# The rows of an expert tile placed in slots four apart

## The reference

```python
g_sel = argmax(t @ rc_w + rc_b)                  # one of 4 groups
lf_sel = (t @ rf_w + rf_b)[g_sel]                # 8 experts of that group
vals, idx = top_k(softmax(lf_sel), 2)            # two of them
for e in range(32):
    h = silu(t @ w_gate[e]) * (t @ w_up[e])      # (536, 512)
    out = out + gates[:, e:e + 1] * (h @ w_down[e])
```

## Time and profile before

| what | value |
|---|---|
| median of three runs | 1102.85 us |
| lowest and highest | 1101.57 and 1104.02 us |
| the profiled execution's own time | 1102.73 us |
| its span, first to last instruction | 1100.9 us |
| mean granted TensorE clock | 0.966 |
| TensorE matmul busy | 992.9 us (90%) |
| VectorE, ScalarE, GpSimd busy | 441.0, 311.5, 330.2 us |
| DMA moved | 277.54 MB, 252 GB/s over the span |

### The profile page before, as it was taken

The page is one execution under the profiler, slowest core; times in us unless marked ns, Lnnn a source line. Parts: engine busy times, 40 slices in busy tenths (PEclk is TensorE's granted clock), DMA queues, the critical chain, the costliest instruction groups (busy, mean ns, idle before and its releaser), DMA issues.

```text
span 1100.9 us, 16994 instructions
## 1 busy us (share of the span) xinstructions
PE 992.9 (90%) x6438; PEld 701.5 (64%) x6439; DVE 441.0 (40%) x674; ACT 311.5 (28%) x597; POOL 330.2 (30%) x534
## 2 busy tenths in 40 slices
PE   6999989999999999999999999999977778998881
PEld 5889768876876587999765555555544434554440
DVE  6999874353435699963151111111101011111103
ACT  3026222453202625322242222222212121221223
POOL 1000888888012994000012222222221111221210
PEclk9999999999979899999989999999989999999996
DMA  6684261110529643327299999999999999999954
GB/s 259 124 146 74 42 141 40 39 60 20 62 79 264 235 150 132 136 96 296 111 359 377 395 392 390 384 393 408 399 393 409 381 421 411 411 417 414 423 237 162
DMA packets 73564, 277.54 MB, mean 252 GB/s; under 512 B 36952, under 2 KB 38872, under 8 KB 56496
## 3 DMA queue, kind: packets, MB, share of 16 engines
q1 hardware_dynamic: 63020, 252.67, 62.6%
q0 software_dynamic: 8720, 19.86, 6.6%
q10 hardware_dynamic: 1780, 4.41, 1.1%
HBM read 260.17 MB, written 25.61 MB: 260 GB/s over the span
## 4 chain that ended last, share of the span: by engine, by line
PE 54%; DMA 22%; DVE 17%; SPq 3%; issue 2%; ACT 1%; POOLq 0%; ACTq 0%; POOL 0%; DVEq 0%
DMA sb_arena<-w_up 16%; PE ps L650 11%; PE ps L1015 8%; PE ps L1008 7%; PE ps L1029 7%; PE ps L912 7%; DVE sb_arena L1386 6%; DMA sb_arena<-w_gate 4%; SPq L407 2%; PE ps L982 2%; PE ps L769 2%; PE ps L795 1%; PE ps L820 1%; PE ps L738 1%; PE ps L816 1%
## 5 line engine op out<-in xcount | busy, mean ns | idle before, releaser
L650 PE MATMUL ps<-sb_arena 128*128 128x264 f32 (+1 forms) x1152 | 273.1, 398 | 14.7 <-DMA sb_arena<-wi 13.8
L650 PEld LDWEIGHTS ps<-sb_arena 128*128 128x128 f32 x1152 | 222.1, 194 | 65.9 <-DMA sb_arena<-wi 13.9
L1889 DVE TENSOR_TENSOR sb_s5b<-sb_s5b,ps 128x256 f32<-128x256 f32 x36 | 22.4, 623 | 414.4 <-PE ps L1015 414.4
L1015 PE MATMUL ps<-sb_arena 128*64 128x256 f32 x1152 | 134.5, 387 | 21.3 <-DMA sb_arena<-w_up 21.3
L1008 PE MATMUL ps<-sb_arena 128*64 128x256 f32 x1152 | 134.3, 387 | 19.1 <-DMA sb_arena<-w_gate 15.0
L1029 PE MATMUL ps<-sb_arena 128*64 128x512 f32 x576 | 131.5, 598 | 20.6 <-DVE sb_arena L1893 20.6
L1008 PEld LDWEIGHTS ps<-sb_arena 128*64 128x64 f32 x1152 | 84.3, 139 | 79.7 <-DMA sb_arena<-w_gate 24.4
L1015 PEld LDWEIGHTS ps<-sb_arena 128*64 128x64 f32 x1152 | 83.6, 139 | 68.3 <-DMA sb_arena<-w_up 27.4
L1359 ACT ACTIVATE sb_kxf<-ps,sb_gate_of 64x512 f32<-64x512 f32 x36 | 24.6, 682 | 304.9 <-PE ps L1029 304.9
L1029 PEld LDWEIGHTS ps<-sb_arena 128*64 128x64 f32 x576 | 39.0, 136 | 90.0 <-issue 61.0
L606 POOL COPY sb_idc<-sb_tok_of 64x1 int32 x36 | 6.4, 178 | 288.5 <-DMA sum_scr<-sb_kxf,sb_rwc 272.4
(11 more groups left out here) (306 smaller groups left out, 1275.0 us busy)
## 6 DMA issues: line engine op xcount, KB each, us to landing
sb_arena<-w_gate SPq DMA_DIRECT2D x32, 2048.0 KB, 32.0
sb_arena<-w_up SPq DMA_DIRECT2D x32, 2048.0 KB, 34.0
sb_arena<-w_down SPq DMA_DIRECT2D x32, 2048.0 KB, 34.3
sb_arena<-wi SPq DMA_DIRECT2D x28, 512.0 KB, 4.1
sb_arena<-w_out SPq DMA_DIRECT2D x4, 2048.0 KB, 8.3
sb_arena<-wglu SPq DMA_DIRECT2D x8, 512.0 KB, 4.6
sb_arena<-ssm_in POOLq DMA_DIRECT2D x8, 512.0 KB, 15.3
o_ssm_s<-sb_arena POOLq DMA_DIRECT2D x8, 512.0 KB, 4.9
```

The lines of the kernel that those rows point to most:

```text
L650: last = mm(ps[:, b0 + h, 0:t1 - t0], ring[w % 3][:, k, :], src[:, k, t0:t1], start=k == 0, stop=k == KD - 1)
L1015: last = mm(ps[64 * r:64 * r + 64, 1, 0:256], xt[:, k, :], Wu[s][:, k, 256 * r:256 * r + 256], start=k == 0, stop=k == KD - 1)
L1889: V.tensor_tensor(hh.rearrange("p (j c) -> p c j", j=2), sg.rearrange("p (c j) -> p c j", j=2), ps[:, 1, 0:256].rearrange("p (c j) -> p c ...
```

## The change

Row r of a tile no longer sits in slot r, but in slot 4 (r mod 16) + r div 16: rows 0, 1, 2, ... 15 in slots 0, 4, 8, ... 60, rows 16 to 31 in slots 1, 5, ... 61, and so on. Only the two comparisons that make `oh_row` are changed. The row number is now compared with a list that is read in another order: the constants 0..63 viewed as (4, 16) and transposed, so that column 4 w + e of the one-hot is compared with 16 e + w. The tokens, the gates and the first tile follow, because all three are products with `oh_row`. The instructions of every engine are the same in number, kind, size and order; what differs is the step of one operand of two VectorE instructions (64 bytes instead of 4 between neighbours), and which of the 64 slots are empty.

```diff
             flat = lambda v: v.rearrange("p i k -> p (i k)")
             io64 = cst[:, C_IO:C_IO + T]
-            tt(oh_row, bc(flat(slf), 2, T), bc(io64, 1, 10), ALU.is_equal)
+            spread = lambda v: v.rearrange("p a (w e) -> p a w e", e=T // 16)
+            row_no = bc(io64.rearrange("p (e w) -> p w e", w=16), 1, 10)
+            rows_at = lambda: tt(spread(oh_row), spread(bc(flat(slf), 2, T)), row_no, ALU.is_equal)
+            rows_at()
             both = oh_row.rearrange("p (i k) t -> p i k t", k=2)
             V.tensor_tensor(oh0, both[:, :, 0], both[:, :, 1], ALU.add).then_inc(oh_first, 1)
             dv.wait_ge(oh_first, 1)
...
             stt(slf, stf, -float(T), slf, ALU.mult, ALU.add)
-            tt(oh_row, bc(flat(slf), 2, T), bc(io64, 1, 10), ALU.is_equal)
+            rows_at()
             tt(oh_tile, bc(flat(stf), 2, IDXC), bc(io64[:, 0:IDXC], 1, 10), ALU.is_equal)
```

## The result

The time after is 1105.81 us (median of 11 runs, 1102.70 to 1108.28), against 1101.98 us for the kernel before (11 runs on the same chip, 1099.32 to 1104.02). The ratio is 1.0033 with a 95% interval of 1.0023 to 1.0044, so the change costs 3.6 us (2.5 to 4.8), the ratio times 1,102 us. The whole interval lies above the 0.2% that a measurement can tell: **slower**, as forecast. The profiled execution took 1105.92 us, with a span of 1104.0 us (before: 1102.73 and 1100.9).

A forecast was written before the change was run, and what follows sets the result against it. The most loaded DMA engine was taken to bound the kernel. 1102.73 us plus 5.2 for ten more rows, minus 0.3 for the last scatter, VectorE and GpSimd 0, gave 1107.6 us; range 1102.5 to 1111.5 us.

The forecast's parts named there:

- The bound: Expert loop: TensorE goes at the pace of the most loaded DMA engine; engines finish up to 22 us apart.
- The mapping: Gathers and scatters: engine g has slots 2g, 2g + 1, 2g + 32, 2g + 33; the last two inferred.
- The price: Token-row packets in the expert loop: ten more rows on the most loaded engine cost 5.2 us, between 3.2 and 5.6.
- Where the time is lost: Expert loop: engine 0 behind from the start, 15.4 us against TensorE's 12.47; longer late periods at 17 to 33 rows.
- The step to a half: End of the loads: DMA share falls in one large step to about 0.5 and stays for 25 us or more.
- VectorE: Two comparisons with a strided operand: 0 us taken, covered by queued loads; 0.7 us kept for the range.
- GpSimd: Waits for scatters in the loop: about 0.6 us longer in tiles of 17 to 32 rows, covered, 0 us.
- The last scatter: End of the kernel: 7 rows on seven engines, one each, so the second round goes away, -0.3 us.
- The sum: Whole kernel: profiled execution plus rows minus last scatter, 1102.73 + 5.2 - 0.3 = 1107.6 us.
- Rival 1: Gathers and scatters: slots in blocks of four on an engine, so the change levels the load; -11.9 us; chance 0.08.
- Rival 2: Expert loop: fewer engines on rows at once hurt weights less, giving back 5 us, so no change; chance 0.12.
- Rival 3: Loop: rows 5.6 us, first comparison 0.7, TensorE's lower clock up to 2, so 1111 us; inside the forecast's range.

The follow-up runs named there:

- level order: Against the kernel before: row r of a tile dealt to engine r mod 16, one row to an engine in turn; 1095.48 us, ratio 0.9933.
- reversed back half: Against the kernel before: rows 0 to 31 keep their slots, the pairs of rows 32 to 63 are put in reverse order; 1092.99 us, ratio 0.9912.
- level, turned on: Against the kernel before: row r of tile t sits where the level order puts row r + 3t, modulo 64; 1091.71 us, ratio 0.9905.
- slots of the change, turned on: Against the kernel before: row r of tile t sits where the change puts row r + 27t, modulo 64; 1091.64 us, ratio 0.9908.
- the last two experiments: Against the kernel before: the slots of the change turned on from tile to tile, 1091.64 us; and the reversed back half, 1092.99 us.

## Why the prediction was right, and where it was not exact

All runs together, in the order of the most loaded engine. The change against before is the ratio times 1,102 us; "loop" is the one profiled execution, first gate product to last down product. That execution is not always a typical one: it lay 4.2 us under its median for the level order and 3.9 us above it for the reversed back half, so these two loops can't be compared with each other; the others lay within 1.5 us of theirs.

| order | greatest load, rows | against before, us | 95% interval | loop, us |
|---|---|---|---|---|
| four neighbours on one engine | 140 | +23.3 | +21.2 to +25.3 | 522.8 |
| slots of the change | 109 | +3.6 | +2.5 to +4.8 | 503.4 |
| the same, plain operand | 109 | +3.7 | +2.4 to +5.0 | 503.6 |
| before | 99 | | | 498.0 |
| slots of before, strided operand | 99 | -0.4 | -2.3 to +1.3 | 497.6 |
| level in the tile | 86 | -7.4 | -9.1 to -5.5 | 490.8 |
| back half reversed | 81 | -9.7 | -12.1 to -7.2 | 492.8 |
| level, turned on | 69 | -10.5 | -12.6 to -8.5 | 489.0 |
| slots of the change, turned on | 69 | -10.1 | -12.1 to -8.3 | 489.4 |

**The bound.** Right. The prediction said that TensorE goes at the pace of the most loaded DMA engine. In nine kernels with the same instructions in the loop and the same bytes the time goes up and down with that one number, from 140 rows to 81. From 81 to 69 rows it falls by 0.8 us only, which the intervals do not tell from nothing; there the loads are nearly level, and presumably the mean of 67 rows and the weights' bytes are the bound, which no run tells apart. The prediction reached this from the 22 us of falling share, and this is where the first look has to go: a mean share of 1.01 says that the engines are all busy, and only the end of the load tells whether they were all needed.

**The mapping.** Right in both halves. The front half was read in the earlier trace rows and is confirmed by the last scatter after (seven engines). The back half was inferred; the last scatter of the order of four neighbours shows it, and the reversed order bears it out. The loads of 109 and 42, 105 and 38 and so on predicted the plateau at a half.

**The price.** The term of the rows was too large. It was put at 5.2 us for ten rows, 0.52 us each, between 3.2 and 5.6. The loop of the one profiled execution grew by 5.46 us, which looks like a hit; but it counts a late start of tile 0 before, without which it is 4.0 us. The medians, which rest on 11 and 12 runs, say 3.6 and 3.7 us for the kernel and for its copy with the plain operand. With the last scatter's -0.3 and nothing for VectorE that leaves 3.9 to 4.0 us for the ten rows, **0.4 us for each** (the interval gives 0.27 to 0.53), between the two ends and nearer the lower one. The prediction had this size in hand: its 0.56 us made a tail of 31 us out of 56 rows, and 22 us were seen, which is 0.39 us a row. It put the difference down to light engines that run dry, but the share was full (1.00 to 1.02) in every window of 25 and 50 us from 575 to 1050 us, so they did not. The tail after says the same, 28 us for 78 rows, 0.36 us. Over larger steps the price is nearer to what was taken: 23.3 us for 41 rows more is 0.57 us each (0.52 to 0.62), 7.4 us for 13 rows fewer is 0.57 us (0.42 to 0.70), 9.7 us for 18 fewer is 0.54 us; and 10.5 us for 30 fewer is 0.35 us again. So one price for all steps is not shown, and why they differ is open. One candidate is that stretches exist in which TensorE is the bound again and rows cost nothing: tiles 26 to 28 go at 12.47 to 12.49 us in both kernels, since tile 26 is the second tile of its expert and needs no weights, and the next experts' weights gain a period by it. That was not tested.

**Where the time is lost.** The prediction had engine 0 behind from the start. TensorE sees none of it for 17 tiles; then the rows show within five tiles. The prediction compared 15.4 us for the weights of an expert with 12.47 us of TensorE for a tile. Per expert TensorE takes 36 / 32 x 12.47 = 14.0 us on the mean, and 15.1 us over the first 17 tiles, so the loads fall behind there by little more than what the rows add. What they lack must come out of the three sets of buffers; no run changed the buffers. The prediction expected longer periods near the end, in tiles of 17 to 33 rows. This was only partly so: tile 17 to 18, with 23 rows, took 17.17 us for 14.66, but the periods from tile 22 on are longer in one place and shorter in another (tile 25: 15.34 us for 16.46, tile 29: 13.45 for 12.47), and the last two are the same.

**The step to a half.** The prediction said one large step to about 0.5 that stays for 25 us or more. The step is there, but in two or three windows (0.82, 0.65, 0.51), and the plateau is 16 us. The whole tail, from the last full window to the end, is about 28 us and was about 22. The even engines are not level among themselves: 109 - 90 = 19 rows are 8 to 11 us of stairs at its end, which the prediction had in its list of loads and left out of its picture.

**VectorE.** Taken at 0, with 0 to 0.7 us in the range. The comparisons took 0.42 us more, within the two bounds. The Trainium skill, in VectorE: DVE Perf Modes, says in "Mode 1× (REGULAR) — the baseline", of the slowest mode that "it makes no assumptions. fp32, weird strides, PSUM operands — all work". That says that such an operand is taken, not that it is as fast; the trace gives the price, 0.83 us became 1.25. The time did not follow (-0.4 us, interval on both sides of 0). The cover that the prediction named, work that is already in the queues, does hold: the share of the DMA engines was 1.01 from 575 to 600 us before and 1.02 after, and the experiment with the strided operand lost 1.7 us at tile 0 and had made it up by tile 18.

**GpSimd.** Taken at 0. Its waits for scatters grew from 272.4 to 286.2 us in the groups, in a loop that is longer as well. That the landing of a single uneven scatter counts for nothing that can be measured is shown by the last two experiments, in which single tiles are about as uneven as before and the time is 10 us lower.

**The last scatter.** Taken at -0.3 us. Its second round is gone as said. The stretch behind the loop became 0.6 us shorter in this pair. Over the nine profiles it is 26.9 to 27.0 us where the 7 rows are on four engines, 26.4 to 26.6 where they are on seven, and 27.6 where they are on two: the term is nearer -0.4 us.

**The sum.** 1102.73 + 5.2 - 0.3 = 1107.6 us, against 1105.8 measured: 1.8 us too much, mostly in the price of the rows; 0.75 us is that the execution it was added to lay above its kernel's median of 11 runs (1102.73 against 1101.98). The measured value lies in the range of 1102.5 to 1111.5 us.

**Rival 1, blocks of four.** It fell as said, by the last scatter. The rule of the Trainium skill, in DMA: Bandwidth & Descriptors, "The descriptor swizzle", is for 128 partitions and puts four neighbours on an engine. For the 64 slots of these gathers and scatters the trace shows pairs; what the two have in common is that the second half of an engine's slots lies 32 further on. What the rival got right is its size: level engines were to give -11.9 us, from the area under the earlier trace rows, and with loads of 65 to 69 rows they gave -10.5 us (8.5 to 12.6).

**Rival 2, fewer engines disturb the weights less.** It was to give back 5 us. From before to the change the rows of a tile go from 11.1 engines in the mean to 10.2. Two kernels with level sums and twice that difference, 13.6 and 11.8 engines, are apart by 0.1 us in the medians, with room for some 3 us in their intervals. A relief of 5 us for the step of the change is thus excluded; one of a microsecond, which would also explain the low price of the ten rows, is not.

**Rival 3.** The upper end of 1111 us was not reached. Of its parts the lower pace of TensorE after waits is there (busy time +1.9 us), but it stands inside the growth of the loop and does not come on top.

## What to carry to other kernels

When all DMA engines are full on the mean, look at the last 20 or 30 us of the load. Here a share that fell in stairs went with one engine as the bound, and a share that fell at once with level engines; the mean work that was left under the stairs was about what levelling gave (12 us forecast, 10.5 measured). Partly filled indirect gathers and scatters loaded the engines unevenly, always the same ones, and the 2 MB weight loads waited for the most loaded; so deal the rows out one to an engine and start each tile at another one. The version that does so needs a list of 64 numbers and four short instructions, and at 1091.7 us it is 1.0% faster than the kernel before and 1.3% faster than the changed one.

## What the runs showed of the hardware

- In an indirect gather or scatter over 64 partitions, four slots lie on each of 16 DMA engines, g with 2g, 2g + 1, 2g + 32 and 2g + 33: seven rows start on four engines in order, on seven in the new slots, on two in slots 0 to 3 and 32 to 34; and the times of nine kernels follow the rows that this rule puts on the most loaded engine.
- A row of 4 KB, gathered and scattered, cost 0.35 to 0.57 us of the kernel's time for each row on the most loaded engine, in steps of 10 to 41 rows, though 4 KB of weights take 0.16 us of an engine.
- A VectorE comparison of 640 elements in float32 took 0.83 us with both inputs plain and 1.24 to 1.25 us when one of them was read in steps of 64 bytes, in two kernels.
- An engine's extra load is not seen in TensorE's periods at first: 17 tiles start at the same times to 0.01 us, and then 5.4 us come within five tiles. In those 17 tiles three are second tiles of an expert and need no weights; that the three sets of buffers cover the rest is argued, not shown.
